# A narrow gate projection rewritten from a column-tiled fp32 product into a split fp32r product, with three weight splits moved ahead of it

## What is computed

```python
def gla_mixer(h, s0, lead, w_in, w_gate, b_gate, g_norm, w_o):   # h = rmsnorm(x, norm_pre_mix[1])
    a = h @ w_in
    q, k, v, r, gd = jnp.split(a, [hk, 2 * hk, 2 * hk + hv, 2 * hk + 2 * hv], axis=-1)
    log_a = jax.nn.log_sigmoid((gd @ w_gate + b_gate).astype(jnp.float32)) / GATE_TAU
    o, s = gla_recurrence(heads(q) * GLA_SCALE, heads(k), heads(v), heads(log_a), s0, lead)
```

## Time and profile before

| | us |
|---|---|
| median of 3 runs | 1591.21 |
| the three runs | 1592.72, 1591.21, 1591.21 |
| the profiled execution: its own time | 1592.72 |
| its span, first to last instruction | 1590.9 |
| PE busy / DVE / ACT / POOL | 1453.5 / 709.8 / 508.8 / 288.0 |
| mean granted PE clock over the span | 0.961 of full |

### The profile page before, as it was taken

One profiled execution on the slowest core, in us unless ns is written; L12 is line 12 of the kernel. 1 busy time (PEld: TensorE's weight loads), 2 busy tenths in 40 slices (PEclk: granted clock), 3 DMA queues, 4 the chain that ended last, 5 costly groups with the idle time before them and its releaser, 6 DMA issues.

```text
span 1590.9 us, 28353 instructions
## 1 busy us (share of the span) xinstructions
PE 1453.5 (91%) x11407; PEld 1309.6 (82%) x11407; DVE 709.8 (45%) x1103; ACT 508.8 (32%) x962; POOL 288.0 (18%) x213
## 2 busy tenths in 40 slices
PE   2877998985989999999999899999978999999997
PEld 2834555553979999999998777788978999999996
DVE  5334666442264334343444645445364334343434
ACT  3133554322253122121223433335264122221223
POOL 5110000000206042140440100000205033150440
PEclk7978999797999999999999899999999999999999
DMA  3620000322313232232321413323212332322321
GB/s 104 164 74 1 1 1 5 87 61 60 91 40 105 81 92 81 80 92 80 92 80 54 122 44 110 98 83 93 81 41 84 89 93 81 91 85 87 93 67 56
DMA packets 210877, 120.22 MB, mean 76 GB/s; under 512 B 22118, under 2 KB 206592, under 8 KB 210784
## 3 DMA queue, kind: packets, MB, share of 16 engines
q1 hardware_dynamic: 206800, 105.73, 23.6%
q0 software_dynamic: 3984, 13.19, 2.4%
HBM read 111.30 MB, written 7.59 MB: 75 GB/s over the span
## 4 chain that ended last, share of the span: by engine, by line
PE 80%; DVE 9%; ACT 5%; issue 2%; DMA 2%; SPq 1%; POOL 0%; DVEq 0%; ACTq 0%; POOLq 0%
PE ps L1763 57%; PE ps L1835 4%; PE ps L1986 2%; PE ps L2022 1%; ACT act_hi L841 1%; PE ps L1945 1%; DVE act_lo L1274 1%; PE ps L2081 1%; DVE x L1268 1%; ACT w_hi L784 1%; DVE w_lo L1229 1%; DVE act_lo L1239 1%; PE ps L2005 1%; PE ps L1969 1%; DMA w_raw<-in_mla_w_in_dram 1%
## 5 line engine op out<-in xcount | busy, mean ns | idle before, releaser
L784 ACT CAST w_hi<-w_raw 128x1024 fp32r<-128x1024 f32 x172 | 180.1, 1049 | 699.1 <-PE ps L1763 661.9
L1763 PE MATMUL ps<-act_hi,w_hi 128*128 128x280 f32 (+1 forms) x1408 | 299.7, 294 | 10.0 <-DVE relu L1511 5.7
L1763 PE MATMUL ps<-act_hi,w_lo 128*128 128x280 f32 (+1 forms) x1408 | 297.0, 292 | 0.0
L1763 PE MATMUL ps<-act_lo,w_hi 128*128 128x280 f32 (+1 forms) x1408 | 296.1, 292 | 0.0
L1229 DVE TENSOR_TENSOR w_lo<-w_raw,w_hi 128x1024 fp32r<-128x1024 f32 x172 | 254.6, 1482 | 79.7 <-ACT w_hi L784 79.7
L1763 PEld LDWEIGHTS ps<-act_hi,w_hi 128*128 128x128 f32 x1408 | 225.4, 191 | 16.4 <-issue 13.9
L1763 PEld LDWEIGHTS ps<-act_hi,w_lo 128*128 128x128 f32 x1408 | 225.6, 190 | 0.0
L1763 PEld LDWEIGHTS ps<-act_lo,w_hi 128*128 128x128 f32 x1408 | 225.0, 191 | 0.0
L1763 PE MATMUL ps<-h_hi,w_lo 128*128 128x280 f32 (+1 forms) x928 | 193.6, 290 | 0.0
L1763 PE MATMUL ps<-h_hi,w_hi 128*128 128x280 f32 (+1 forms) x928 | 192.9, 289 | 0.0
L1763 PE MATMUL ps<-h_lo,w_hi 128*128 128x280 f32 (+1 forms) x928 | 192.7, 289 | 0.0
(11 more groups left out here) (324 smaller groups left out, 1986.8 us busy)
## 6 DMA issues: line engine op xcount, KB each, us to landing
w_raw<-in_mlp_w_up_dram SPq DMA_DIRECT2D x64, 512.0 KB, 4.1
w_raw<-in_mlp_w_down_dram SPq DMA_DIRECT2D x64, 512.0 KB, 4.2
w_raw<-in_gla_w_in_dram SPq DMA_DIRECT2D x24, 512.0 KB, 3.9
pg_ckv<-in_cache_ckv_dram SPq DMA_DIRECT2D x64, 128.0 KB, 2.1
w_raw<-in_mla_w_o_dram SPq DMA_DIRECT2D x8, 512.0 KB, 4.2
sts<-in_state_gla_dram POOLq DMA_DIRECT2D x4, 1024.0 KB, 6.6
out_dram<-sts POOLq DMA_DIRECT2D x4, 1024.0 KB, 5.8
w_raw<-in_gla_w_o_dram SPq DMA_DIRECT2D x8, 512.0 KB, 4.3
```

What stands on the lines that cost most here:

```text
L784: nc.scalar.copy(w_hi[slot(g)][:], w_raw[raw_slot(g)][:]).then_inc(w_rounded, 1)
L1763: last = nc.tensor.matmul(out[:, h, 0:n], w[:, c, :], a[:, c, t0 + n * h:t0 + n * h + n], start=(c == 0 and k == 0), stop=(c == DC - 1 and ...
```

## The change

The gd product becomes a split fp32r product like the others: 48 matmuls of 280 tokens with 16 output columns, no column groups. ACT rounds the 16 columns into `gd_hi` behind its three rounds of weights; DVE subtracts into `gd_lo`. The result is read in one operation in place of four. On DVE the three splits of q1, k1 and v2 move from behind the gd work to ahead of it, to the end of `first_items`.

```diff
-                gd_w = sb_in(s2, "gd_w", [P, DC, RANK])
+                gd_hi = sb_in(s2, "gd_hi", [P, DC, RANK], F32R)
+                gd_lo = sb_in(s2, "gd_lo", [P, DC, RANK], F32R)
@@ ScalarE
             next_weights("q0")
             next_weights("k0")
             next_weights("v0")
+            act.wait_ge(gd_in, 16)
+            nc.scalar.copy(gd_hi[:], gd_raw[:]).then_inc(tail_rounded, 1)
             gate_log(0)
@@ VectorE, end of first_items
+                for t in ("q0", "k0", "v0"):
+                    next_weights(t)
@@ VectorE
             first_items()
-            dve.wait_ge(gd_in, 16)
-            nc.vector.tensor_tensor(gd_w[:], gd_raw[:], gain[:, R_PRE_MIX + DC:R_PRE_MIX + 2 * DC].rearrange("p (c o) -> p c o", o=1)
-                                    .to_broadcast([P, DC, RANK]), ALU.mult).then_inc(tail_split, 1)
-            gd_rows = projected("gd")
-            for q in range(4):
-                last = nc.vector.tensor_tensor(gdT[:, T // 4 * q:T // 4 * (q + 1)], gd_rows[32 * q:32 * q + RANK, 0, 0:T // 4],
-                                               rstd_pre[32 * q:32 * q + RANK, T // 4 * q:T // 4 * (q + 1)], ALU.mult)
-            last.then_inc(blk_read, 1)
-            for t in ("q0", "k0", "v0"):
-                next_weights(t)
+            dve.wait_ge(tail_rounded, 2)
+            nc.vector.tensor_tensor(gd_lo[:], gd_raw[:], gd_hi[:].bitcast(F32), ALU.subtract).then_inc(tail_split, 1)
+            nc.vector.tensor_tensor(halves(gdT[:]), projected("gd")[0:RANK], halves(rstd_pre[0:RANK, :]), ALU.mult)\
+                .then_inc(blk_read, 1)
             gate_min(0)
@@ TensorE
             pair_free("gd")
             pe.wait_ge(tail_split, 2)
-            for c in range(DC):
-                for q in range(4):
-                    last = nc.tensor.matmul(item_ps("gd")[32 * q:32 * q + RANK, 0, 0:T // 4], gd_w[:, c, :], x[:, c, T // 4 * q:T // 4 * (q + 1)],
-                                            start=(c == 0), stop=(c == DC - 1), tile_position=(0, 32 * q))
-            last.then_inc(blk_mm, 1)
+            product(item_ps("gd")[0:RANK], (gd_hi, gd_lo), (act_hi, act_lo), 0, HALF).then_inc(blk_mm, 1)
             gate(0)
```

## The result

The changed kernel took 1605.47 us (median of 4, 1603.01 to 1606.43), and the old one beside it 1591.97. The ratio is 1.008, with a 95% interval of 1.0062 to 1.0098. Run again beside other kernels it gave 1605.52 and a ratio of 1.0086 (1.0073 to 1.0099), that is 11.6 to 15.8 us. Forecast was slower by 8.2 us (1599.4), with a range up to 1602.5; the measured time lies above it. The direction and the path of the wait were right, the size was too small. The profiled execution took 1603.25 (span 1601.4).

What follows compares the result with a forecast made beforehand. PE's order was taken to bound the kernel (busy 91% of the span, 80% of the chain). v1's delay of 13.5 us less 5.4 coming back gave +8.2 on 1591.21, so 1599.4, range 1595.5 to 1602.5.

Steps and rivals of the forecast that it cites:

- The wait for v2 on gd's path: Before gd on PE: gd must wait until v2 has landed, been rounded and split, starting at 901.3 instead of 891.9.
- The transfer: v2's weight load, issued at 892.74 beside two state loads: 3.88 us plus 2.0, landing at 898.6.
- The upper end: v2's load: data ready at about 894.9 with 2.3 us of state data to go, so at most 2.3 lost.
- served after the states: Case for v2's load: its data move only after the two states' data, losing 2.3 us.
- sharing: Case for v2's load: equal shares of time with the states turn its 1.7 us of data into 3.4.
- rule of round robin between queues: DMA engines alternate packets between queues with work, so v2's landing is slowed as assumed; always served first, it lands at 896.6.
- The product: New gd product on PE: 6.34 us plus 2.0 for a half-clock start (bounds 1.6 and 2.6), 8.3 in all.
- the rival of the cheap product: gd on PE: 48 narrow matmuls at 58 ns take 2.8 us, giving +2.7, 1593.9; chance 0.04.
- The estimate of 5.7: gd product on PE: the skill's full-clock spacing of 119 ns for 48 matmuls gives 5.7 us, set aside for 6.34.
- v1 at half clock: Rival at block v1, behind gd and G0: the clock falls and v1 costs +1.5, giving 1600.9; chance 0.20.
- What comes back: From v1's start to q1's end, 5.4 us regained: 1.5 on v1, 2.3 of waiting, 1.6 on q1.
- The sum: At q1's end: v1's delay of 13.5 less 5.4 coming back, +8.2 us, reaching the kernel's end, 1599.4.

Runs made afterwards that it cites:

- Experiments 1: Old kernel with the splits of q1, k1 and v2 moved ahead of gd_w, old column-tiled product kept: 1599.21 us, ratio 1.0051.
- 6: Changed kernel with only the q1 and k1 splits ahead of gd, v2's split behind the reading of gd, gd_hi ahead of v2's rounding: 1595.12 us, ratio 1.0016.
- experiment 3: Changed kernel with GpSimd loading the two GLA states only once gd_lo has been made: 1600.15 us, ratio 1.0051.
- 4: Changed kernel with 76 filler matmuls of 280 columns in TensorE's wait for gd_lo: 1601.75 us, ratio 1.0063.
- 7: Old kernel with the q1 and k1 splits between gd_w and the reading of gd, v2's split behind it: 1589.03 us, ratio 0.9972.
- 13: Changed kernel unaltered, profiled a third time: 1607.34 us.
- 2: Changed kernel's new product with the splits left behind the reading of gd, gd_hi rounded ahead of v2: 1596.97 us, ratio 1.0028.
- 8: Old kernel with q1 and k1 splits under the old product, and gate 0 put ahead of v2 on ScalarE and VectorE: 1588.96 us, ratio 0.9976.
- 11: Kernel 8 with 18 filler matmuls in TensorE's wait for gd_w: 1586.17 us, ratio 0.9957 against the old kernel.
- 12: Changed kernel with the states loaded behind gd_lo and 50 filler matmuls in TensorE's wait: 1599.47 us, ratio 1.0038.
- experiment 5: Changed kernel unaltered, run again beside other kernels: 1605.52 us, ratio 1.0086.

## Why the forecast was right in kind and too small

**The wait for v2 on gd's path: right.** gd's first matmul came behind gd_lo, at 902.82, after an idle time of 13.5 us, through split, transfer, rounding and split as forecast. Experiments 1 and 6 show it from both sides: the move alone costs 7.1 us in the stretch, and taking back the third split gives 7.7.

**The transfer: the step that failed most.** I wrote "I take +2.0, and keep 0 and 2.3 as the ends". It measured 7.34 - 3.88 = +3.5, and 3.5 again by experiment 3. The upper end was wrong in its construction. I took the 2.2 us of the transfer that aren't data as a wait ahead of the data, so that v2's data would start at about 894.9 and have 2.3 us of states left in front of them. In the trace of before only 1.0 us lies between issue and first packet. So v2's data could have started at 893.8, and they started at 896.9, when the states were nearly through as I had said. That is +3.1, the case "served after the states" with the right start. The +2.0 that I took stood for sharing, and the queues show no sharing: nothing of the weights moved up to 896.9. I named the second load (v3's, released by k1's split) nowhere, but it wasn't the cause: experiment 3 had it too, at 3.83. The last 0.4 us, between first packet and landing (3.2 against 2.8), weren't tried apart.

The Trainium skill's rule of round robin between queues, a packet at a time ("DMA: Bandwidth & Descriptors", Queues, rings and completion order), isn't borne out here in the sense in which I used it. By turns v2 would have had packets between 893.8 and 896.9, and it had none. Kernels 1, 4, 7 and 13 show the same: v2 asked for while the states moved, its first packet 3.8 to 4.2 us later, the transfer 7.1 to 7.4. Whether all that was left of the states counted as one turn can't be seen in a trace.

**The product: right, a little dear.** Forecast 8.3, measured 7.76, and 6.31 at full clock (row of layer 0: 6.34). So half clock cost 1.5 us, where I had 2.0 and a lower bound of 1.6: only 3.2 us of the product ran at 0.50. 16 columns are as slow as 32 or 128, so the rival of the cheap product fell. The estimate of 5.7 from the Trainium skill's spacing was too low here ("TensorE: Matmul & The Clock Gate", Back-to-back issue gap): 6.31/48 is 131 ns each. The page gives that spacing for a single matmul by itself, and this product is a stream with a weight load to each.

**v1 at half clock: the second step that failed.** I gave it 0.20, as a rival of +1.5, and let v1 take 6.37. It took 7.90. It did so in every kernel of this study whose gd began at half clock or fell to it (the old one, the changed one, 1, 2, 3, 6, 7, 8), and in none of 4, 11 and 12, where gd ran at full clock. The filler is what was changed between the two groups, so what went on ahead of gd decides about v1 too. The rows of before already showed one such case; I set too much by the shorter pause between gd and G0 (0.82 us, forecast 0.9).

**What comes back: right.** q1 waited 1.0 behind v1 and took 6.43. Forecast was 13.7 us from v1's start to q1's end. It measured 15.3, which is 13.8 and the 1.5 of v1's half clock.

**The sum.** 1.5 too little for the transfer, 1.5 for v1, 0.5 too much for the product make the 2.5 us by which the stretch missed (+10.7 against +8.2). Behind it the chain is as before: from q1's end to the last instruction it is 673.7 us before and 673.5 after. So the delay does reach the end in full, as said. The median of the result lies 6.1 us above the forecast: these 2.5, another 2.8 outside the stretch (1.6 in experiment 5), and 0.8 by which the old kernel itself was slower than in the runs shown at first. The part outside the stretch goes with a lower mean clock, as said above; why the changed kernel has it stays open. My range had room for one more half-clock stretch on top of v1's, from a base of 1591.2. The old kernel itself ranged from 1587.2 to 1597.5 over the study's runs, so three runs were too narrow a base.

## What to carry to other kernels

Before work is moved in an in-order queue, ask what the moved work itself waits for: the split of v2 waited for a load that only the splits ahead of it could release, and everything behind it inherited that wait. Move the part that releases a load forward, and leave the part that waits for it behind whatever is urgent. When that brings a load forward, also see what else is moving then: asked for 5.4 us earlier, v2 landed only 1.9 us earlier, because the states went first. Ask when the first packet of such a load can move, not only when it is issued. A narrow fp32 product in four column groups can be cheaper than a split product that costs as much as a full block. Where TensorE must pause by a chain of other engines, a few matmuls on data that is already there can pay for themselves, if they end before the wait does.

## What the runs showed of the hardware

- A 512 KB load took 3.7 to 3.9 us with no other queue's load moving, its first packet 1.0 us behind the issue. Asked for while two 1 MB loads of another queue were moving, it took 7.1 to 7.4 us, and its first packet came only when they were nearly through, 3.8 to 4.2 us behind the issue.
- A split product of 48 matmuls by 280 columns took 6.3 to 6.4 us at 2.4 GHz with 16, 32 and 128 weight columns. The same 16 columns in plain fp32, 32 matmuls of 140 in four column groups, took 2.1 us at full clock and 3.3 to 3.8 when it began at half clock or soon fell to it.
- What went on ahead of a product showed in the clock of the next one. In the changed kernel gd began at half clock and was at full clock again from 906.0, and still v1 was granted 1.2 GHz for part of its time. With filler ahead of gd, the same pause of 1.34 us as in the old kernel and the same small product behind it left the clock at 2.4. 18 useless matmuls in 2.7 us of a wait saved about 3 us of the kernel's time.
